# Two-tile stage ends of a transformer stack: the next norm applied as rows ahead of the transposes, and its parts split straight from PSUM

## The reference

```python
sh_m, sc_m, gt_m, sh_f, sc_f, gt_f = jnp.split(mod[:, None, :], N_MOD, axis=-1)
h = rms_norm(x, g_pre_mix[l]) * (1.0 + sc_m) + sh_m
y = token_mixer(h, w_in[l], ...)
x = x + gt_m * rms_norm(y, g_post_mix[l])
h = rms_norm(x, g_pre_ffn[l]) * (1.0 + sc_f) + sh_f
y = conv_glu_ffn(h, ...)
x = x + gt_f * rms_norm(y, g_post_ffn[l])
```

## Time and profile before

| | us |
|---|---|
| runs of the kernel | 2558.19, 2557.23, 2554.05 |
| median | 2557.23 |
| span of the profiled execution, first to last instruction | 2550.9 |
| TensorE busy in it | 2414.4 (95%) |
| VectorE, ScalarE, GpSimd busy | 1744.7, 1080.0, 384.1 |
| mean granted TensorE clock | 0.985 of full |

### The profile page before, as it was taken

One profiled execution on the slowest core, in us unless ns is written; L12 is line 12 of the kernel. 1 busy time (PEld: TensorE's weight loads), 2 busy tenths in 40 slices (PEclk: granted clock), 3 DMA queues, 4 the chain that ended last, 5 costly groups with the idle time before them and its releaser, 6 DMA issues.

```text
span 2550.9 us, 34427 instructions
## 1 busy us (share of the span) xinstructions
PE 2414.4 (95%) x13098; PEld 2025.5 (79%) x13098; DVE 1744.7 (68%) x2562; ACT 1080.0 (42%) x1850; POOL 384.1 (15%) x431
## 2 busy tenths in 40 slices
PE   3889999889999999999979999999999999998998
PEld 3678987779988878877648887888888888777997
DVE  6967887957995776776966475675575676356554
ACT  3466554566554212226745322224322225344543
POOL 1101111011111100104861110100100100001101
PEclk9999999999999999999989999999999999999999
DMA  8655986546783664552212263443353454322662
GB/s 316 219 170 193 296 305 221 194 144 215 256 274 121 200 198 140 186 187 84 66 42 83 84 194 138 155 171 119 114 200 115 165 182 115 116 80 87 190 198 91
DMA packets 135876, 422.46 MB, mean 166 GB/s; under 512 B 28448, under 2 KB 32672, under 8 KB 135712
## 3 DMA queue, kind: packets, MB, share of 16 engines
q1 hardware_dynamic: 135152, 418.55, 48.6%
q10 hardware_dynamic: 560, 1.72, 0.2%
HBM read 419.11 MB, written 1.11 MB: 165 GB/s over the span
## 4 chain that ended last, share of the span: by engine, by line
PE 61%; DVE 5%; ACT 2%; issue 1%; POOL 1%; DVEq 0%; POOLq 0%; ACTq 0%
PE ps L1149 19%; PE ps L1151 19%; PE ps L1150 19%; PE ps L1344 2%; DVE sl L1695 1%; PE ps L1332 1%; DVE F L1813 1%; POOL ap L2227 1%; DVE mjunk L1709 1%; ACT F L1466 1%; PE ps L1312 1%; PE ps L1301 0%; DVE ps L2052 0%; PE ps L1367 0%; PE ps L1249 0%
## 5 line engine op out<-in xcount | busy, mean ns | idle before, releaser
L1149 PE MATMUL ps<-hH,sh 128*128 128x256 f32 (+1 forms) x2560 | 841.1, 329 | 7.9 <-DVE hL L1784 3.5
L1150 PE MATMUL ps<-hL,sh 128*128 128x256 f32 (+1 forms) x2560 | 835.8, 326 | 0.0
L1151 PE MATMUL ps<-hH,sl 128*128 128x256 f32 (+1 forms) x2560 | 835.8, 326 | 0.0
L1407 ACT ACTIVATE sh<-raw 128x1024 fp32r<-128x1024 f32 x534 | 541.1, 1040 | 419.9 <-PE ps L1151 312.7
L1695 DVE TENSOR_TENSOR sl<-raw,sh 128x1024 fp32r<-128x1024 f32 x534 | 644.4, 1232 | 79.9 <-ACT sh L1407 79.4
L1709 DVE CUSTOM_DVE_ANT_0 mjunk<-raw,cB,V 128x1024 bf16<-128x1024 f32 x384 | 543.1, 1414 | 32.5 <-DMA C<-in_cst 8.4
L1149 PEld LDWEIGHTS ps<-hH,sh 128*128 128x128 f32 x2560 | 481.4, 188 | 61.2 <-issue 9.9
L1150 PEld LDWEIGHTS ps<-hL,sh 128*128 128x128 f32 x2560 | 481.7, 188 | 49.4 <-issue 1.7
L1151 PEld LDWEIGHTS ps<-hH,sl 128*128 128x128 f32 x2560 | 481.6, 188 | 48.1
L2200 POOL TENSOR_TENSOR uLl<-F,uHh 128x256 fp32r<-128x256 f32 (+1 forms) x132 | 163.4, 1238 | 1188.2 <-ACT uHh L1584 1090.5
L1149 PE MATMUL ps<-sh,uHh 128*128 128x512 f32 x792 | 312.7, 395 | 9.5 <-DVE sl L1695 9.2
(11 more groups left out here) (165 smaller groups left out, 2107.9 us busy)
## 6 DMA issues: line engine op xcount, KB each, us to landing
raw<-in_w SPq DMA_DIRECT2D x752, 512.0 KB, 4.6
G<-gates SPq DMA_DIRECT2D x14, 512.0 KB, 7.1
raw<-in_w SPq DMA_DIRECT2D x16, 256.0 KB, 4.0
cB<-in_rpb SPq DMA_DIRECT2D x64, 64.0 KB, 2.6
raw<-in_w SPq DMA_DIRECT2D x4, 492.0 KB, 6.2
S<-in_rows SPq DMA_DIRECT2D x6, 256.0 KB, 3.2
X<-in_x ACTq DMA_DIRECT2D x1, 1024.0 KB, 11.8
X<-in_ctx SPq DMA_DIRECT2D x1, 1024.0 KB, 8.4
```

What stands on the lines that cost most here:

```text
L1149: self.e.matmul(out, lh, rh, start=start, stop=False)
L1150: self.e.matmul(out, lh, rl, start=False, stop=False)
L1151: return self.e.matmul(out, ll, rh, start=False, stop=stop)
L1407: self.e.activation(self.m["sh"][k % SPL][:, 0:w], self.m["raw"][r % RAW][:, 0:w], ACT.Copy).then_inc(self.sems["w_hi"], 1)
```

## The change

It has these parts.

1. **Rows.** `spread_coefs` adds two SyncE steps. `rsend` writes A and B (8 columns of 128 each) to DRAM, two element-wise writes like a gate's; `rfetch` waits for them and reads both as rows repeated on all partitions into X[:, 2] and X[:, 3], tiles that are free then. They are put in `aside` behind the step that makes A (`coef`), which moves earlier: in the mixers from the end of the attention to its middle, in feed-forward 0 by four paces, in the neighbourhood attention from its end to the product of v.
2. **Norm.** `norm_rows` takes the place of `norm_tile` at the four ends. VectorE computes z = x A for both halves (`zrow`) as soon as X is there, and then h = z rs + B (`hrow`) when rs is there. The transposes follow, and `hsplit` reads PSUM itself; the steps L1750, L1447, L1768 and L1466 are gone there.
3. **Order.** In `gate_half` tile 0's two splits come one behind each `gate2` of tile 1. In feed-forward 0 tile 0's transposes and splits came before tile 1's gate, and now they follow that order too. A step `lowers` puts waiting `lower` steps ahead of tile 1's last half (mixers) or of its gate (the other two), and `ahead` sets the 6 of the running maximum to 2 from tile 1's last steps on, and back to 6 in the next stage.
4. **Filler.** 14 and 5 `warm` matmuls become 9 and 3 at three openings. Mixer 1 opens with 4 (before 8), takes tile 1's norm ahead of the unit (7, 3) of tile 0, with no more warm matmuls after.
5. **Context load.** `ctx_load` (X[:, 2:4] and two vectors) stood behind the last `w_ada` unit, inside feed-forward 1. It now comes right after mixer 1 and waits for the rows' last reader; `need("w_ada", 1, 5)` is called ahead of it.

```diff
+    def spread_coefs(self, AB, streams_gone=()):
+        rid = self.new()
+        self.add("rsend", AB=AB, id=rid)
+        self.add("rfetch", id=rid, before=self.spread, gone=list(streams_gone))
+        self.spread = rid
+        return rid
+    def norm_rows(self, hid, t, rid, st):
+        self.rms_more(st, self.xs(t, 1))
+        ys = [self.place("S", 2 + j) if t else self.next("PT", 2) for j in range(2)]
+        self.add("zrow", t=t, ys=ys, rid=rid, xs=[self.xs(t, 0), self.xs(t, 1)])
+        self.rms_close(st, 2)
+        self.add("hrow", t=t, ys=ys, rid=rid, st=st)
+        def first():
+            parts = []
+            for g in range(2):
+                b = self.bank()
+                p = dict(src=ys[g], ready=("y", ys[g]), b=b, f=None, k0=4 * g, i=t, on=None, hid=hid, id=self.new())
+                self.add("turn", p=p)
+                parts.append(p)
+            def second(p):
+                self.add("hsplit", p=p)
+                self.left(p["b"])
+            self.seconds += [lambda p=p: second(p) for p in parts]
+        self.firsts.append(first)
...
     def down(...):
+                    if close and half and i and u == 2:
+                        self.add("ahead", n=2)
...
-                if i and lead:
-                    self.first_parts()
-                    self.second_parts()
+                if close and half and i:
+                    self.add("lowers")
                 done(t, half, banks[i])
...
     def gate_half(...):
             self.add("gate2", ...)
             if j == 0:
                 st = self.rms_open(self.xs(t, 0), D)
-        self.norm_tile(hid, t, AB, 0, st, early=True)
+            if rid:
+                self.second_part()
+        self.norm_tile(hid, t, AB, 0, st, early=True, rid=rid)
...
     def mixer(...):
         for i in range(2):
-            if i:
+            if i and not l:
                 self.finish_norms()
                 self.warm(4)
+            elif i:
+                self.add("ahead", n=AHEAD)
             elif l:
-                self.warm(8)
+                self.warm(4)
...
+                    if l and not i and (cb, u["at"]) == (7, 3):
+                        self.finish_norms()
...
         for i in tiles:
+            if i:
+                self.add("ahead", n=2)
             for half in range(2):
+                if i and half:
+                    self.add("lowers")
...
+    def open_two(self):
+        self.warm(9)
+        self.finish_norms()
+        self.warm(3)
+        self.add("ahead", n=AHEAD)
...
         h = self.mixer(1, h, ab1(1, 3, "g_pre_ffn"))
+        self.need("w_ada", 1, 5)
+        self.add("ctx_load", before=self.spread)
...
+    def rsend(self, s):
+        AB = s["AB"]
+        a = self.m["A"][:, AB["ab"] * 16:AB["ab"] * 16 + 8]
+        self.wait_ge(self.got("A", AB["id"]))
+        self.mods(AB["name"], AB["l"], AB["vshift"], 1)
+        self.wait_ge(self.own("rw"))
+        for k, col in enumerate((a, self.mcol(AB["name"], AB["l"], AB["vshift"]))):
+            dst = bass.AP(tensor=self.dram["gates"].tensor, offset=(2 + k) * D, ap=[[1, P], [P, 8], [1, 1]])
+            self.e.dma_start(dst, cut(col, [list(col.ap[1]), [1, 1]]), allow_slow_non_contiguous=True).then_inc(
+                self.sems["rs"], 16)
+            self.landed("rs", *([("rsent", s["id"])] if k else []))
+    def rfetch(self, s):
+        self.wait_ge(self.got("rsent", s["id"]))
+        if s["before"]:
+            self.wait_ge(self.got("rows_left", s["before"]))
+        for key in s["gone"]:
+            self.wait_ge(self.got(*key))
+        for k in range(2):
+            src = bass.AP(tensor=self.dram["gates"].tensor, offset=(2 + k) * D, ap=[[0, P], [1, D]])
+            self.e.dma_start(self.m["X"][:, 2 + k, :], src).then_inc(self.sems["rw"], 16)
+            self.landed("rw", *([("row", s["id"])] if k else []))
...
+    def zrow(self, s):
+        for j, y in enumerate(s["ys"]):
...
+            self.e.tensor_tensor(self.buf(y)[:, :], self.m["X"][:, s["t"], c], self.m["X"][:, 2, c], ALU.mult).then_inc(
+                self.sems["v_sb"], 1)
+    def hrow(self, s):
...
+            self.e.scalar_tensor_tensor(self.buf(y)[:, :], self.buf(y)[:, :], rs, self.m["X"][:, 3, c], ALU.mult,
+                                        ALU.add).then_inc(self.sems["v_sb"], 1)
```

More of the change, by code:

```diff
@@ L267, in o_piece, with down @@
         self.add("hsplit", p=p)
-    def down(self, w, act, nk, k0, tiles, done, c0=0, lead=False):
+    def down(self, w, act, nk, k0, tiles, done, c0=0, close=False):
         for half in range(2):
@@ L318, in products, with gate_half @@
         return [b for _, b in got]
[L320 removed]
+    def gate_half(self, t, half, b, gid, AB, hid, st2, rid=None):
         if half == 0:
@@ L604, in later @@
             AB[0] = ab_next()
-        self.aside += [lambda: None] * (5 if l else 9) + [later]
+        self.aside += [lambda: None] * 5 + [later]
+        if l == 0:
+            self.aside.append(lambda: rid.append(self.spread_coefs(AB[0])))
         self.down(("w_down", l), ("u1", fid), KF, 0, [0, 1],
-                  lambda t, half, b: self.gate_half(t, half, b, gid, AB, hid, st2), lead=l == 0)
+                  lambda t, half, b: self.gate_half(t, half, b, gid, AB, hid, st2, rid), close=l == 0)
         self.flush()
@@ L774, in na @@
         gid = self.gates_later("mod_w_2", l, 5, 1.0, 1, True)
+        AB, rid = [], []
+        gone = [("y", y) for y in self.wide_ys]
+        self.aside += [lambda: AB.append(ab_next()), lambda: rid.append(self.spread_coefs(AB[0], gone))]
         nid = self.new()
@@ L847, in na @@
         self.flush()
-        self.down(("na_w_o_2", (0,)), ("h", h1), KD, 0, [0, 1], done)
+        self.down(("na_w_o_2", (0,)), ("h", h1), KD, 0, [0, 1], done, close=True)
         self.u_at += 1
@@ L908, in finish @@
         out, n, ctx, top, used, order, lower, loads = [], 0, False, 0, set(), [], [], []
+        ahead = AHEAD
         for s in self.steps:
+            if s["kind"] == "ahead":
+                ahead = s["n"]
+                continue
+            if s["kind"] == "lowers":
+                out += lower
+                lower = []
+                continue
             real = "unit" in s and s["kind"] != "place"
@@ L914, in finish @@
             if "unit" in s or "upto" in s:
-                top = max(top, s["upto"] if "upto" in s else s["unit"] + 1 + (AHEAD if real else 0))
+                top = max(top, s["upto"] if "upto" in s else s["unit"] + 1 + (ahead if real else 0))
                 while n < min(top, len(self.units)):
@@ L932, in finish @@
                 loads.append(s["unit"])
-                if job == ("w_ada", 1, 47):
-                    out.append(dict(kind="ctx_load"))
                 continue
@@ L1681, in __init__ @@
                           glu1_b=self.glu1_b, glu2_a=self.glu2_a, cglu_v=self.cglu_v, tap_v=self.tap_v, ln_sq=self.ln_sq, ln_rstd=self.ln_rstd,
-                          ln_out=self.ln_out, qk2=self.qk2, v2=self.v2, final=self.final_scale)
+                          ln_out=self.ln_out, qk2=self.qk2, v2=self.v2, final=self.final_scale,
+                          zrow=self.zrow, hrow=self.hrow)
     def start(self, s):
@@ L1744, in rs @@
         return self.m["st"][:, st["i"] * 4 + 3:st["i"] * 4 + 4]
+    def zrow(self, s):
+        for j, y in enumerate(s["ys"]):
+            self.wait_ge(self.got("row", s["rid"]))
+            self.wait_ge(self.gone(y))
+            self.x_ready(s["xs"][j])
+            c = slice(j * 512, (j + 1) * 512)
+            self.e.tensor_tensor(self.buf(y)[:, :], self.m["X"][:, s["t"], c], self.m["X"][:, 2, c], ALU.mult).then_inc(
+                self.sems["v_sb"], 1)
+            self.done("v_sb", ("z", y))
+    def hrow(self, s):
+        rs = self.rs(s["st"])
+        for j, y in enumerate(s["ys"]):
+            self.wait_ge(self.got("row", s["rid"]))
+            self.wait_ge(self.got("z", y))
+            c = slice(j * 512, (j + 1) * 512)
+            self.e.scalar_tensor_tensor(self.buf(y)[:, :], self.buf(y)[:, :], rs, self.m["X"][:, 3, c], ALU.mult,
+                                        ALU.add).then_inc(self.sems["v_sb"], 1)
+            self.done("v_sb", ("y", y), ("rows_left", s["rid"]))
     def scale(self, s):
```

48 lines of the change are left out of this document (29 added, 19 removed).

## The result

The changed kernel takes **2565.33 us** (median of 15 runs, 2560.80 to 2576.29) against 2557.80 us for the kernel before (15 runs, 2553.08 to 2564.94): ratio 1.003, 95% interval 1.002 to 1.004. It is 7.5 us slower, where 2.7 us faster was forecast; the time lies above the forecast's range (2547 to 2561).

A forecast was written before the change was run, and what follows sets the result against it. TensorE is busy 95%; the stage ends were taken as chains over ScalarE, GpSimd and VectorE. Full-clock gains of -6.5 us, plus 2.3 and 1.5 for clock falls, gave -2.7: 2554.5 us, range 2547 to 2561.

The forecast's parts named there:

- The three would have cost nothing later, beside products: Mixer 1's end: three modulation units pulled ahead of tile 1's low parts eat the gain, +0.3 us; later they were free.
- `ctx_load` ... nothing: Mixer 1's end: the context load holds SyncE until the three units end, costing nothing with eight loads ahead.
- Mixer 0 (-2.7): Mixer 0's end: evacuation and a modulation unit leave the chain, so the first matmul comes at 218.05, 2.7 us sooner.
- E: End of tile 1's first `gate2`, where the new chain starts; forecast at 210.4 us in mixer 0.
- only then the second `gate2` (E + 2.65): New chain on VectorE: tile 0's first low part, waiting for ScalarE, precedes tile 1's second `gate2`, ending at E + 2.65.
- Feed-forward 0 (-2.2, +2.3 for the clock, up to 2 for SyncE): Feed-forward 0's end: tile 1's products 2.2 us sooner; clock fall costs 2.3; loads queued behind `rsend` up to 2.
- Neighbourhood attention (-2.2): Neighbourhood attention's end: first matmul at 2360.8 against 2363.01, 2.2 us sooner.
- Rival 3: Rows late because element-wise writes don't overlap, VectorE waiting in mixers 0 and 1; 2571 us, chance 0.07.
- The clock (+3.8): Longer TensorE idle at the openings lowers the clock: 2.3 us at feed-forward 0's end, 1.5 over the other three.
- Rival 1: All ends: gains come in full and the clock is kept; 2547 to 2552 us, chance 0.33.
- Rival 2: Clock falls at every opening, the removed filler being what kept it; 2557 to 2561 us, chance 0.15.
- Rival 4: `ahead` = 2 can't lower an already raised maximum; worth 0 in three of four ends, in the sum; no chance given.

The follow-up runs named there:

- e7: Kernel before with the change at mixer 1's end alone, including the three modulation units and context load; 2562.8 us, ratio 1.0029.
- e10: Kernel before with only units 45 to 47 and the context load drawn ahead at mixer 1's end, old norm and fillers; 2562.6 us, ratio 1.0022.
- e9: Kernel before with the change at mixer 1's end alone, next three modulation-unit steps of the second feed-forward let pass; 2559.2 us, ratio 1.0017.
- e11: Whole change at all four ends, with the next three modulation-unit steps after mixer 1 let pass; 2555.9 us, ratio 1.0001 to the kernel before.
- e17: Kernel before with the change at mixer 0's and neighbourhood attention's ends, tile 0's splits behind tile 1's row norm in mixer 0; 2556.5 us, ratio 0.9993.
- e18: As e17, but three low parts and not four ahead of the softmax in mixer 0; 2554.0 us, ratio 0.9979 to the kernel before.
- e15: Kernel before with the change at mixer 0's end alone, tile 0's splits behind tile 1's row norm; 2555.5 us, ratio 0.9997.
- e5: Kernel before with the change at mixer 0's end alone; 2557.8 us, ratio 1.0003.
- e8: Kernel before with the change at the neighbourhood attention's end alone; 2552.5 us, ratio 0.9991.
- e2: Changed kernel with the running maximum one lower in mixer 0's attention, so three low parts stand ahead of the softmax; 2563.1 us, ratio 1.0020 to before.
- e3: Changed kernel with the three modulation units and context load behind tile 1's low parts at mixer 1's end; 2566.2 us, ratio 1.0026 to before.
- e1: Changed kernel with the row fetch six steps behind the column sending in feed-forward 0's down stage; 2564.7 us, ratio 1.0025 to before.
- e16: The kernel before, unchanged, profiled a second time; 2552.9 us, span 2550.7 us.
- e4: Changed kernel with the fillers of the kernel before restored (14 and 5, and 8 at mixer 1's start); 2569.3 us, ratio 1.0040 to before.

## Why the prediction was wrong, step by step

Forecast and measured time lie 10.2 us apart (-2.7 and +7.5). By the ratios of the single ends, good to 2 or 3 us each, some 7.1 of it is mixer 1's end, 3.5 mixer 0's and 1.4 feed-forward 0's, the neighbourhood attention's is right, and 1.8 comes off for the clock and the rows, which stood in the sum apart.

**The step that failed is in mixer 1**: the three units priced at their own place alone, as in "The three would have cost nothing later, beside products". The chain itself I had nearly right: less the 11.1 us of drift that came before, the first product stood at 584.5, forecast 584.0. But I counted the three units only where they went. What follows them in the queue of modulation units moved up by three, and those are the two-stream units, 2.56 us of VectorE each instead of 1.28, in a stage in which VectorE has 9.3 to 9.9 of 10 us busy. I had the cover in the wrong place: "beside products" covers TensorE's time, not VectorE's. Mixer 1's end as a whole costs 0.29% (7.4 us, e7), forecast +0.3, and the three units with the context load alone 0.22% (e10). What letting three steps pass takes back is 0.12% at this end alone (e7 to e9, 3 us, intervals overlapping) and 0.29% in the whole change (to e11, 7.4 us). So the queue that moves up is worth 3 to 7 us, and the runs don't bound it closer. In the changed kernel's profile the 6.85 us are 0.9 for the opening's chain, 4.0 from the first product to 665 us, where the 4.5 us of waits for low parts lie, 0.3 up to 720, and 1.6 behind that at half clock, which e17 and e18, whose mixer 1 ends as before, lose there too. "`ctx_load` ... nothing" was not tried by itself; e11 keeps it and shows no wait for a weight's low part up to 665 us.

**Mixer 0 (-2.7).** Three parts. E came as forecast: 214.01 less the drift of 3.77 is 210.2, forecast 210.4. The modulation unit's leaving gave 1.4, as said. The chain from E was longer: transposes at E + 5.85 and not 5.2 (GpSimd's power came 0.6 later), the first product 3.04 behind them at half clock and not 2.45. And the moved unit "costs nothing" where it went in VectorE's time, which is so (173.11 us, in idle time), but it takes a number in the plan, so that a fourth weight part is readied ahead of a softmax. That this costs some 3.2 us (mean of 3.9 in eleven profiles, less 0.7 in six) is an estimate: 1.1 of it, the low part itself, is in every one of the eleven, and the half clock behind the longer wait is the rest.

**The order of the chain** I had read and not questioned: "only then the second `gate2` (E + 2.65)". In e15's profile turning it round was worth 3.7 us of opening against e5's. The prediction took the sequence as given, priced it nearly right, and so missed what could be won there.

**Feed-forward 0 (-2.2, +2.3 for the clock, up to 2 for SyncE).** Less drift, tile 0's products began at 409.8 (forecast 410.15) behind 4.55 us of idle time, and the clock fell, as said; tile 1's came 0.3 earlier, not 2.2, as the clock term has it. The down stage, where columns and rows travel, lost 1.4 to 5.0 us, about my upper bound and above; I had put them at nothing in the sum. Some 0.8 us more goes in mixer 1's start, in all nine profiles with this end changed, which I had not counted. And the first profile flattered the kernel before here: behind that wait of 1.9 us six of the eight profiles that have it fell to half clock and lost some 1.3 us, which this one did not.

**Neighbourhood attention (-2.2).** Right in mechanism and size: -2.20 in the changed kernel, -2.21 in e8. In e2 and e3 the clock fell at this opening and only 0.65 and 0.76 us were left of it.

**Rows late.** Right that they are not, or hardly: in mixer 0 `zrow` ran without a wait in eleven of thirteen profiles and waited 0.78 and 0.96 us for its rows in e1 and e2, within the 0 to 2.5 of the prediction. Rival 3 is out.

**The clock (+3.8).** Its sign was right, its places only partly. In the changed kernel idle times of 3.92 and 4.55 us were followed by half clock and 2.49 us was not, but 2.51 us at mixer 1's end was. The Trainium skill, "TensorE: Matmul & The Clock Gate", section "HAM oscillation — how this bites in real kernels", says idle gaps make the array start cold; the long ones agree, in every profile that has them (seven with 3.58 to 3.93 us at mixer 0's opening, eight with 4.25 to 4.57 at feed-forward 0's end). For the short ones the prediction leaned on one execution: "one idle time of 1.9 that keeps the full clock". In e16, the same program, TensorE's clock is full over that idle time too and falls soon behind it, where the first profile's stays full; e16's two stretches, then the first profile's second:

```profile
404.30:408.20 3.90, 2.00 (x11) 1.45 (x9) 3.13 (x7) 2.93 (x8) 0.00 (x0) 1.00 0.91 297
408.20:412.20 4.00, 4.00 (x21) 4.00 (x22) 2.47 (x4) 1.60 (x6) 1.40 (x5) 0.59 0.24 97
```

```profile
408.80:412.80 4.00, 3.95 (x32) 3.98 (x33) 2.52 (x4) 1.65 (x6) 1.34 (x5) 1.00 0.29 118
```

The clock fell behind this 1.9 us in six of eight profiles, behind the 2.4 to 2.5 us of the neighbourhood attention's end in two of eleven, and behind the 1.57 us of the openings with the splits behind in none of five. So the length of one idle time, by which I judged, does not tell it alone, and one execution does not tell it for a program. What does is open.

**The rivals.** Rival 1 (clock kept, gains in full) holds at the neighbourhood attention's end alone, and there in nine of eleven profiles. Rival 2 (2557 to 2561) had the sign, by the wrong mechanism, and e4 shows that the old filler is no remedy. Rival 4 was in the sum and was not tried by itself. None of the four had the queue that moves up.

## What to carry to other kernels

When work is pulled ahead in a queue that is filled at a rate, the price is not only where it lands: everything behind it in that queue moves up too, so ask what kind of work that is and which engine is full there. When a chain sets the end of a stage, look through it for steps that another tile put in between; moving those behind the last link was worth 3 us in the profile of that opening, more than shortening the links. And change one end at a time where several can be: four such kernels told what the whole change's profile could not.

## What the runs showed of the hardware that was not expected

With TensorE busy throughout and a granted clock of 1.00, one execution holds 172 matmuls in 20 us and another 179. The changed kernel, then the second profile of before, both in 253 to 273 us:

```profile
253.00:273.00 20.00, 20.00 (x172) 20.00 (x172) 16.92 (x26) 10.80 (x17) 3.02 (x3) 1.00 0.72 238
```

```profile
253.00:273.00 20.00, 20.00 (x179) 20.00 (x178) 19.11 (x29) 12.05 (x19) 3.43 (x3) 1.00 0.78 285
```

Over the up stage the drift came out near -1.5, 0 to 0.3, or 3.1 to 3.5 us in nearly all profiles, in kernels with and without the change. What sets it stays open; it is as large as the effects studied here, so no verdict rests on it.

The two 4 KB element-wise writes in the first feed-forward took 14.2 and 15.3 us to land in the changed kernel and 10.6 to 13.5 us in the eight other profiles that have them, against a median of 10.5 for the gates' in the earlier trace rows. In the changed kernel SyncE, which waits for them, issued no weight load for 15.6 us, and eight loads ahead were not enough: VectorE waited 5.93 us for one.

Two executions of one program can differ in whether the clock falls behind the same idle time, as the two profiles of before do at 408 us.
